# Value columns of both halves multiplied in two stages of the opening of a 16-stage transformer kernel; eight head slots in place of nine

## The reference

```python
c_act = jax.nn.silu(c)
mod = (c_act @ ada_w[layer] + ada_b[layer])[:, None, :]
sh_a, sc_a, gt_a, sh_m, sc_m, gt_m = jnp.split(mod, 6, axis=-1)
h = modulate(rms_norm(x, attn_norm[layer]), sh_a, sc_a)   # rms_norm * (1 + sc_a) + sh_a
q, k, v = jnp.split(h @ w_in, 3, axis=-1)                 # 8 heads: q, k of 2 x 64, v of 128
# per head: a = softmax(q1 k1 + bias) - lambda * softmax(q2 k2 + bias);  o = a @ v
# o = rms_norm(o, subln) * (1 - lam_init);  x = x + gt_a * (o @ w_out)
```

## Time and profile before

| | |
|---|---|
| median of 3 runs | 1409.15 us (1406.42 to 1410.65) |
| profiled execution, its time | 1413.62 us |
| span in the profile | 1411.8 us |
| TensorE busy | 1320.3 us, 94% of the span |
| VectorE busy | 872.8 us, 62% |
| ScalarE busy | 679.5 us, 48% |
| GpSimd busy | 171.2 us, 12% |
| read from HBM | 264.83 MB, 188 GB/s over the span |
| TensorE idle from 40 to 160 us | 16.5 of 120 us |

### The profile page before, as it was taken

One profiled execution on the slowest core, in us unless ns is written; L12 is line 12 of the kernel. 1 busy time (PEld: TensorE's weight loads), 2 busy tenths in 40 slices (PEclk: granted clock), 3 DMA queues, 4 the chain that ended last, 5 costly groups with the idle time before them and its releaser, 6 DMA issues.

```text
span 1411.8 us, 22238 instructions
## 1 busy us (share of the span) xinstructions
PE 1320.3 (94%) x8582; PEld 1140.6 (81%) x8582; DVE 872.8 (62%) x1546; ACT 679.5 (48%) x1196; POOL 171.2 (12%) x172
## 2 busy tenths in 40 slices
PE   6797999999999999999999878999999998899999
PEld 2687899888889855789898765799998776799987
DVE  2768578888667377695545675565555554645443
ACT  2454554343554346454445575554444555554442
POOL 0546011100100000010000130011010101011000
PEclk9889999999999899999999999999999999999999
DMA  9967639899868433269655262198655454376660
GB/s 350 314 219 241 193 105 311 301 312 341 298 185 229 146 120 91 82 196 281 189 182 158 87 191 61 61 229 251 182 177 180 134 180 119 102 203 184 184 179 31
DMA packets 249225, 267.43 MB, mean 189 GB/s; under 512 B 11040, under 2 KB 185376, under 8 KB 248736
## 3 DMA queue, kind: packets, MB, share of 16 engines
q1 hardware_dynamic: 246496, 263.52, 60.1%
q10 hardware_dynamic: 2624, 2.49, 0.5%
HBM read 264.83 MB, written 1.15 MB: 188 GB/s over the span
## 4 chain that ended last, share of the span: by engine, by line
PE 56%; DVE 7%; ACT 4%; issue 2%; POOL 1%; ACTq 0%; DMA 0%; DVEq 0%; POOLq 0%
PE bank L558 10%; PE bank L560 9%; PE bank L559 9%; PE ps_s L558 3%; PE ps_s L559 3%; PE ps_s L560 3%; PE ps_p L559 3%; PE ps_p L558 3%; PE ps_p L560 3%; DVE wlo L1564 2%; ACT whi L2661 2%; PE ps_s L1273 1%; POOL rs L3288 1%; PE ps_p L1139 1%; PE ps_s L1103 1%
## 5 line engine op out<-in xcount | busy, mean ns | idle before, releaser
L1564 DVE TENSOR_TENSOR wlo<-wring,whi 128x1024 fp32r<-128x1024 f32 (+1 forms) x376 | 456.2, 1229 | 231.0 <-ACT whi L2661 229.2
L2661 ACT ACTIVATE whi<-wring 128x1024 fp32r<-128x1024 f32 (+1 forms) x376 | 388.5, 1043 | 353.7 <-PE ps_p L560 123.2
L558 PE MATMUL bank<-h_hi,whi 128*128 128x256 f32 x1216 | 351.7, 289 | 4.7 <-DVE h_lo L1739 2.3
L559 PE MATMUL bank<-h_lo,whi 128*128 128x256 f32 x1216 | 347.8, 286 | 0.0
L560 PE MATMUL bank<-h_hi,wlo 128*128 128x256 f32 x1216 | 347.5, 286 | 0.0
L558 PEld LDWEIGHTS bank<-h_hi,whi 128*128 128x128 f32 x1216 | 237.3, 195 | 10.7 <-issue 7.4
L559 PEld LDWEIGHTS bank<-h_lo,whi 128*128 128x128 f32 x1216 | 237.3, 195 | 0.7
L560 PEld LDWEIGHTS bank<-h_hi,wlo 128*128 128x128 f32 x1216 | 237.1, 195 | 0.0
L3326 POOL TENSOR_TENSOR ex<-ex 128x512 f32<-128x512 f32 x64 | 72.4, 1131 | 714.3 <-ACT g_hi L2792 714.3
L1807 DVE TENSOR_TENSOR g_lo<-ex,g_hi 128x512 fp32r<-128x512 f32 x64 | 44.2, 690 | 125.9 <-POOL ex L3326 125.7
L558 PE MATMUL bank<-whi,h_hi 128*128 128x512 f32 (+3 forms) x248 | 100.5, 405 | 15.2 <-DVE h_lo L1685 6.2
(11 more groups left out here) (394 smaller groups left out, 1886.4 us busy)
## 6 DMA issues: line engine op xcount, KB each, us to landing
wring<-in_mlp_w SPq DMA_DIRECT2D x128, 512.0 KB, 5.2
wring<-in_ada_w SPq DMA_DIRECT2D x96, 512.0 KB, 7.2
wring<-in_mlp_w_in SPq DMA_DIRECT2D x64, 512.0 KB, 4.7
wring<-in_mlp_w_out SPq DMA_DIRECT2D x64, 512.0 KB, 4.1
wring<-in_a_w_in SPq DMA_DIRECT2D x24, 512.0 KB, 5.7
wring<-in_moba_w_qkv SPq DMA_DIRECT2D x24, 512.0 KB, 3.9
wring<-in_kv_ada_w SPq DMA_DIRECT2D x16, 512.0 KB, 7.6
wring<-in_w_kv SPq DMA_DIRECT2D x12, 512.0 KB, 5.2
```

The costliest lines, as they stand in the source:

```text
L558: nc.tensor.matmul(out, lh, rh, start=first, stop=False)
L559: nc.tensor.matmul(out, lh, rl, start=False, stop=False)
L1564: v.tensor_tensor(piece_view(wlo, p), raw_view(p), piece_view(whi, p).bitcast(F32), ALU.subtract).then_inc(lo_ready, 1)
L2661: a.activation(piece_view(whi, p), raw_view(p), ACT.Copy).then_inc(hi_ready, 1)
```

## The change

The opening chunks come in the order 2, 0, 3, 1. Scale and shift of K-tiles 0 to 3 (chunks 2 and 0) are ready first; the transposes are made in two groups, K-tiles 0 to 3 of both token tiles and then 4 to 7, and between the rows of chunks 3 and 1 TensorE multiplies K-tiles 0 to 3 of both value halves. K-tiles 4 to 7 of both follow the second split. The value slot is gone. The matrix-vector parts of chunks 4 to 7, of which four were done in the opening and four in the value slot, are now two pairs in each head slot, and the four loads of chunk 8 lie together behind head 0's.

```diff
-HEAD_OF_SLOT = (0, 1, 2, 3, None, 4, 5, 6, 7)
-MOD_SLOTS = (1, 4, 5)
+MOD_SLOTS = (2, 4, 6)
...
 def slot_piece(s):
-    return 4 + 2 * s + (2 if s > 4 else 0)
+    return 8 + 2 * s
...
-    plan += ada(0, (2, 3, 0, 1))
-    plan += [a_v_part(0, 0), a_v_part(0, 1), ada_part(4, 0), a_v_part(0, 2), ada_part(4, 2), a_v_part(0, 3),
-             ada_part(4, 4), ada_part(8, 0), ada_part(4, 6)]
-    for h in range(4):
-        plan += a_qk(h) + [ada_part(6, 2 * h), ada_part(*((8, 2 + 2 * h) if h < 3 else (9, 0)))]
-    for j in range(4):
-        plan += [a_v_part(1, j), ada_part(5, 2 * j)]
-    for h in range(4, 8):
-        plan += a_qk(h) + [ada_part(7, 2 * h - 8)]
-        if h < 7:
-            plan += [ada_part(9, 2 * h - 6)]
+    plan += ada(0, (2, 0)) + [a_v_part(0, 0), a_v_part(0, 1)] + ada(0, (3,)) + [a_v_part(1, 0)] + ada(0, (1,))
+    plan += [a_v_part(1, 1)] + [a_v_part(c, j) for c in range(2) for j in (2, 3)]
+    for h in range(8):
+        plan += a_qk(h)
+        if h == 0:
+            plan += ada(0, (8,))
+        if 3 <= h < 7:
+            plan += [ada_part(9, 2 * h - 6)]
+        c, k = (4, 6, 5, 7)[h // 2], 4 * (h % 2)
+        plan += [ada_part(c, k), ada_part(c, k + 2)]
...
             pe.wait_ge(sem("c_ready"), 1)
             ada_rows(0)
+            pe.wait_ge(sem("ident_in"), 16)
+            turn_opening(0)
+            ada_columns(0)
+            ada_rows(1)
+            ada_columns(1)
+            v_banks = [token_banks(("a_v", 0))]
+            pe.wait_ge(sem("a0_split"), 2)
+            token_piece(("a_v", 0), v_banks[0], h, False)
+            ada_rows(2)
+            token_piece(("a_v", 0), v_banks[0], h, False)
+            ada_columns(2)
+            pe.wait_ge(mod_drained, 2)
+            turn_opening(1)
+            v_banks.append(token_banks(("a_v", 1)))
+            token_piece(("a_v", 1), v_banks[1], h, False)
+            ada_rows(3)
+            ada_columns(3)
+            token_piece(("a_v", 1), v_banks[1], h, False)
+            pe.wait_ge(sem("a0_split"), 4)
+            for c in range(2):
+                for j in (2, 3):
+                    token_piece(("a_v", c), v_banks[c], h, j == 3)
...
-            for j in range(4):
-                matvec(matvec_order[0], 2 * j, 2 * j + 2)
-                keep_ahead("dve", j)
+            keep_ahead("dve", 3)
             dve.wait_ge(sem("bias_in"), 16)
-            for s in range(9):
-                head = HEAD_OF_SLOT[s]
+            for s in range(8):
                 p = slot_piece(s)
                 keep_ahead("dve", p)
                 if slot_head(s - 1) is not None:
                     diff_scores(slot_head(s - 1))
                 if slot_head(s - 3) is not None:
                     diff_even(slot_head(s - 3))
-                if head is None:
-                    for j in range(4):
-                        matvec(matvec_order[2], 2 * j, 2 * j + 2)
-                        keep_ahead("dve", p + j)
-                else:
-                    matvec(matvec_order[1 if head < 4 else 3], 2 * (head % 4), 2 * (head % 4) + 2)
+                for k in (4 * (s % 2), 4 * (s % 2) + 2):
+                    matvec(matvec_order[s // 2], k, k + 2)
                     keep_ahead("dve", p + 1)
```

More of the change, by code:

```diff
@@ L830, in ada_columns, with turn_opening @@
                 last.then_inc(sem("early_columns"), 1)
[L832 to L848, removed]
+            def turn_opening(half):
+                for t in range(TT):
+                    if half == 0:
+                        pe.wait_ge(sem("normed"), t + 1)
+                        use = ("a0", "turn", 2 * t)
+                        to = bank[:, bank_take(pe, use), :]
+                        piece_of[use] = -1
+                    else:
+                        to = odd_turned[t]
+                    for i in range(4):
+                        j = 4 * half + i
+                        last = nc.tensor.transpose(to[:, i * P:(i + 1) * P], xn[:, t, j * P:(j + 1) * P], ident[:, :])
+                    last.then_inc(filled[uses["a0", "turn", 2 * t][0]] if half == 0 else sem("odd_turned"), 1)
             def token_banks(key):
@@ L971, in _ @@
                     diff_scores(slot_head(s - 1))
[L972 to L976, removed]
+                qk_piece(s, b, 1)
+                if s == 7:
+                    gate_rows("a0", 16)
                 if slot_head(s - 3) is not None:
@@ L2071, in _ @@
                     gate("a0")
-            p = slot_piece(9)
+            p = slot_piece(8)
             keep_ahead("dve", p)
@@ L2795, in mlp, with opening_sums @@
                 keep_ahead("act", first_piece[(f"{tag}_w2", 7)])
-            for c in range(4):
+            def opening_sums(c):
                 act.wait_ge(sem("early_rows"), c + 1)
                 a.activation(early_sums[c], early_banks[c], ACT.Copy).then_inc(sem("early_sums"), 1)
+            opening_sums(0)
+            keep_ahead("act", 0, 1)
+            opening_sums(1)
+            keep_ahead("act", 1, 1)
+            opening_sums(2)
+            keep_ahead("act", 2, 1)
             act.wait_ge(sem("lam_dots"), 1)
@@ L2807, in _ @@
             for t in range(TT):
-                split_turned("a0", t, [(h_hi, h_lo, gs, mod[:, 0:8])])
-                keep_ahead("act", t, 1)
+                f, part = whole(2 * t + 1, 0), tile_part(2 * t + 1, 4)
+                act.wait_ge(sem("odd_turned"), t + 1)
+                for i in range(4):
+                    ins = a.activation(f[:, i, :], odd_turned[t][:, i * P:(i + 1) * P], ACT.Identity,
+                                       scale=gs[:, 4 + i:5 + i], bias=mod[:, 4 + i:5 + i])
+                ins.then_inc(sem("act_done"), 1)
+                n_act[0] += 1
+                act.wait_ge(sem("act_done"), n_act[0])
+                a.activation(h_hi[part], f, ACT.Copy).then_inc(sem("a0_high"), 1)
+            keep_ahead("act", 3)
             def diff_copy(u):
@@ L2850, in diff_high @@
                     sem("diff_high"), 1)
-            for t in range(TT):
-                drain(("a_v", 0, "tok", t), v_tok[:, t, 0:W], (0, W))
+            for c in range(2):
+                for t in range(TT):
+                    drain(("a_v", c, "tok", t), v_tok[:, t, c * W:(c + 1) * W], (0, W))
             act.wait_ge(sem("subln_ready"), 1)
-            for s in range(9):
-                head = HEAD_OF_SLOT[s]
+            for s in range(8):
                 p = slot_piece(s)
@@ L2863, in _ @@
                 keep_ahead("act", p + 1)
[L2864 to L2868, removed]
+                drain(("a_qk", s), qk_t[:, s, :], (0, W), ROOT_EIGHTH)
                 if slot_head(s - 3) is not None:
```

50 lines of the change are left out of this document (28 added, 22 removed).

## The result

The changed kernel took **1435.62 us** (median of four runs, 1432.08 to 1437.88), the kernel before 1409.06 on the same chip: ratio 1.0176, 95% interval 1.0152 to 1.0201. The two medians are 26.6 us apart; the ratio makes it 24.8. The forecast was 1425 with a range up to 1434, so the median lies 1.6 us above the range: the sign and the places were right, the size was too small, 16 us.

The account below looks back on a forecast made before the run. SyncE's in-order load ring, waiting on VectorE's matrix-vector steps, was taken to pace the head slots while TensorE waits. Head 6's reductions 14.0 later plus tail 2.0 gave +16.0 on 1409.15, so 1425 us, range 1410 to 1434.

Parts of the forecast that it names:

- What bounds the kernel: Head slots: TensorE waits for weights, paced by SyncE's in-order ten-slot queue, which waits 56.8 us for VectorE's matrix-vector steps.
- Opening, +1.8: Start of kernel: multiplying beside the loads hides nothing net; late odd halves make the opening cost 1.8 us.
- GpSimd as a lock, slot 1 at 87.5: Chunk 8: its four loads hold the queue until GpSimd frees them at 80, so slot 1's reductions start at 87.5.
- the middle: GpSimd's eight chunk 8 steps: 24.5 us taken, between 21.4 from the shortest rows and 27.4.
- Circle, 66.8: Slot 1 to slot 6: query halves wait for the second matrix-vector part; five turns of 12.1 to 14.1, together 66.8 us.
- the 3 us of the prediction: Five turns and slot 1: by the skill page's 3.2 us transfer instead of 3.8, they would be 3 us shorter.
- "With 2 us of slack": Head slot turns of 12 to 14 us: a lower TensorE clock after holes was counted as costing nothing.
- the step of 9.3: From slot 6's reductions to head 6's in slot 7, which waits for no late load: 7.1 plus 2.2, 9.3 us.
- Tail, +2.0: After the head slots: gate rows move behind head 6's scores, costing 2.0 us; the rest of the tail unchanged.
- the forecast +14.0: Head 6's reductions begin at 163.6 against 149.61 before, 14.0 us later.
- Rival (a): Whole head stretch: the queue keeps up, TensorE has no holes, 1394 us, faster; chance 0.12.

Follow-up runs that it names:

- run 2: Changed kernel with the same loads issued in the order in which VectorE and GpSimd use them: 1404.6 us, ratio 0.9950 to the kernel before.
- run 7: Changed kernel with loads in order of use, but chunk 8's four loads together behind head 0's halves: 1406.5 us, ratio 0.9954 to the kernel before.
- run 8: Changed kernel with both column halves of each head moved one slot earlier, all blocks kept: 1412.7 us, ratio 1.0000 to the kernel before.
- run 3: Changed kernel with the opening of the kernel before, all eight value pieces behind it: 1425.0 us, ratio 1.0088 to the kernel before.
- run 1: Changed kernel with chunk 8's four loads spread over three head slots instead of together: 1436.6 us, ratio 1.0163 to the kernel before.
- run 4: Changed kernel with both matrix-vector pairs of a slot ahead of VectorE's second low split: 1440.1 us, ratio 1.0190 to the kernel before.
- run 6: Changed kernel with the opening of the kernel before and its loads in order of use: 1404.0 us, ratio 0.9934 to the kernel before.

## Why the prediction was right in sign and too small in size

- **What bounds the kernel**: right. SyncE's in-order ring paces the head slots; runs 2, 7 and 8 move nothing but the order of loads and give 31, 29 and 23 us back.
- **Opening, +1.8**: the forecast times were 0.6 to 1.6 early (30.26 against 29.7, 54.12 against 52.9, 55.75 against 54.2), and so the second four pieces start 3.0 us after the point of before (52.72). The forecast effect, nothing hidden net, holds. What the opening does at the end was said to come through GpSimd, and does, but by its load behind the bias and not by the odd halves, and was undersized: run 3 prices it at 10.6 us.
- **GpSimd as a lock, slot 1 at 87.5**: the mechanism is there (83.86, then 83.89, then 84.30), and run 3 moves both by 6.9 us. The size failed, and it is the largest term of the miss: I chose the middle between the short and the long steps, 24.5, because "VectorE is idle for part of that time", and they took 27.4, the long end. VectorE was idle for 12.0 us of it (59.70 to 63.17, 64.44 to 68.58, 72.49 to 76.85), and there a step is 1.57 us; what I left out is that its work comes in bursts, and one burst makes one step 3.53:

```profile
62.67 1.57 POOL L3326 TENSOR_SCALAR xn<-wring,c_col 128x512 f32<-128x512 f32 x1
...
63.17 1.27 DVE L1574 TENSOR_TENSOR wlo<-wring,whi 128x1024 fp32r<-128x1024 f32 x1 [3.47 <-ACT whi L2675]
68.58 3.91 DVE L1574 TENSOR_TENSOR wlo<-wring,whi 128x1024 fp32r<-128x1024 f32 x3 [4.14 <-ACT whi L2675]
```

  The Trainium skill's rule of one shared SBUF pair with an exclusive lock (SBUF — State Buffer, SBUF: two separate sides) agrees with the 3.53 beside the three low splits at 68.58 and the 1.57 without them. It doesn't account for the step at 62.67, which stays at 1.57 though a low split starts inside it and takes 1.27, so the lock can't be priced from the overlap alone. The start was 1.0 late, the way from GpSimd's end to the reductions 8.25 instead of 7.5. Together 4.6 us: slot 1 at 92.11. What I didn't see is the second lock at the same time (run 1), so that spreading chunk 8 alone would have gained nothing.
- **Circle, 66.8**: 68.1 measured (12.1, 14.0, 14.2, 14.2, 13.5 for 12.1, 13.5, 14.1, 14.1, 13.0), its landings of 5.5 us included, forecast as 3.8 plus 1.36. In run 4 they take 7.5. The Trainium skill's fit (DMA: Bandwidth & Descriptors, Anatomy of one DMA — SWDGE (gpsimd) path), which is for loads issued by GpSimd, has 3.2 for the first part. The shortest way that I read here, from SyncE's issue to ScalarE's start, is 3.75 us (run 8, 77.93 to 81.68), so the trace disagrees; and six landings that are 0.6 us shorter would have been 3.6 us, not the 3 of the prediction.
- **"With 2 us of slack" the clock costs nothing**: this step failed. After a hole of 3.2 us, to 162.09, and 2.3 us of small matmuls (granted clock 0.75) the 24 products of a piece run from 164.42 at a granted clock of 0.50, the lower level of 1.2 GHz:

```profile
164.42 0.56 PE L557 MATMUL bank<-h_hi,whi 128*128 128x256 f32 x1
...
169.69 0.68 PE L946 MATMUL ps_p<-ident,ex 128*128 128x128 f32 x3
```

  5.3 us, where the next 24 (171.15 to 174.13) take 3.0 at a granted clock of 1.00, 2.4 GHz. In slots 1 to 6 the clock is low too (0.66 over 95 to 110 us), but the turns come out as the ring sets them; between slots 6 and 7 no late load covers it, and the step of 9.3 is 11.1: +1.8. Run 3 bears this out: there the hole ahead of the same piece is 1.96 us, the piece runs at 1.00 (155.94 to 159.06), and the step is 8.9.
- **A wait not forecast**: VectorE does head s-1's even step (L2054) behind the reductions that the late split holds up, so TensorE waits at the difference turned back as well, 14.1 us in four. It adds nothing to the turn, which the ring sets, but it makes the hole in front of the slow piece.
- **Tail, +2.0**: from head 6's reductions to the first residual 36.55 us against 35.64, +0.9; behind it +1.7. Sum: 4.6 + 1.3 + 1.8 on top of the forecast +14.0, and 2.6 for 2.0 at the tail: 24.3.
- **Rival (a)**, a queue that keeps up, was priced at 1394. Runs 2, 6 and 7 come closest to that case, at 1404 to 1407: the holes don't all close, since slot 1 starts at 78 to 81 and the turns stay at 9 to 13 us, most likely by VectorE's work.

## What to carry to other kernels

A ring that one queue fills in order should be filled in the order in which its buffers are *needed*, with whatever paces the kernel a slot ahead of loads whose buffers come free at a slot's end; ask for every load that matters which load it reuses, and which loads stand in front of it and what they wait for. When two locks open at about the same time, taking one away shows nothing: run 1 looks like a refutation of GpSimd's lock and is none. Run 4 is another case: the work ended earlier and the load landed later. And a sum that takes "the middle" between an engine alone and beside its neighbour should first ask which of the neighbour's instructions fall into that stretch.

## What the runs showed of the hardware that was not expected

A 512 KB load issued by SyncE took 5.5 us to landing with one such load just ahead of it and 7.5 in a kernel that frees two at once. A hole of some 3 us was followed by a piece at a granted clock of 0.50, 5.3 us instead of 3.0. A GpSimd multiply of 128x512 took 1.57 us alone and 3.53 beside three low splits on VectorE, but 1.57 too with one low split of 1.27 us starting inside it.
